# Input LayerNorm and the split of layer 0's W_IN moved from a stage of their own into the first projection stage

## What is computed

```python
hp = layer_norm(concatenate([meta, x_prompt]), in_ln_g, in_ln_b)
hs = layer_norm(x_sample, in_ln_g, in_ln_b)
for l in range(2):
    z = einsum('btd,de->bte', h, w_in[l])          # 1024 -> 1184
    cq, ckv, kr, sq, sk, sv = split(z)             # then RMS norms and rotary embedding of the parts
    # latent attention, sliding-window attention, W_OUT, LayerNorm,
    # SwiGLU FFN (2816 wide), LayerNorm
```

## Time and profile before

| | us |
|---|---|
| median of 3 runs | 3561.3 (3555.37 to 3571.3) |
| the profiled execution | 3558.67 |
| its span, first to last instruction | 3556.9 |
| PE busy | 3131.2 (88%) |
| DVE busy | 1603.1 (45%) |
| ACT busy | 847.7 (24%) |
| POOL busy | 829.7 (23%) |
| mean granted clock of PE, share of 2.4 GHz | 0.926 |

### The profile page before, as it was taken

One profiled execution on the slowest core, in us unless ns is written; L12 is line 12 of the kernel. 1 busy time (PEld: TensorE's weight loads), 2 busy tenths in 40 slices (PEclk: granted clock), 3 DMA queues, 4 the chain that ended last, 5 costly groups with the idle time before them and its releaser, 6 DMA issues. The chain is left out here.

```text
span 3556.9 us, 46203 instructions
## 1 busy us (share of the span) xinstructions
PE 3131.2 (88%) x18240; PEld 2848.6 (80%) x18240; DVE 1603.1 (45%) x2904; ACT 847.7 (24%) x1612; POOL 829.7 (23%) x675
## 2 busy tenths in 40 slices
PE   0978887889899999999859688878889999999995
PEld 0966665767899999999749566667669999999995
DVE  6447777546322222222355577756562222222226
ACT  1323333621311111111123233345121111111111
POOL 1222333621211121111012133345111211111211
PEclk9988998779999999999969898977999999999997
DMA  5221112621211011110133211045121111111101
GB/s 196 86 89 45 31 31 69 178 75 67 71 36 35 35 53 41 41 41 24 51 103 108 74 39 31 25 124 153 62 74 42 49 46 41 41 35 35 37 22 66
DMA packets 122002, 222.70 MB, mean 63 GB/s; under 512 B 33408, under 2 KB 74624, under 8 KB 121168
## 3 DMA queue, kind: packets, MB, share of 16 engines
q1 hardware_dynamic: 111072, 189.22, 16.5%
q0 software_dynamic: 10800, 31.73, 2.3%
HBM read 174.40 MB, written 42.46 MB: 61 GB/s over the span
## 5 line engine op out<-in xcount | busy, mean ns | idle before, releaser
L2166 PE MATMUL PS<-xh,fwh 128*128 128x390 f32 (+1 forms) x2112 | 719.0, 340 | 6.7 <-DVE fwl L2110 6.7
L2167 PE MATMUL PS<-xl,fwh 128*128 128x390 f32 (+1 forms) x2112 | 723.0, 342 | 0.0
L2168 PE MATMUL PS<-xh,fwl 128*128 128x390 f32 (+1 forms) x2112 | 722.1, 342 | 0.0
L2134 DVE TENSOR_TENSOR acc<-acc,PS 128x390 f32<-128x390 f32 x528 | 295.8, 560 | 494.0 <-PE PS L2168 494.0
L2121 DVE TENSOR_TENSOR gate<-PS,gate 128x390 f32<-128x390 f32 x132 | 74.4, 564 | 747.5 <-PE PS L2168 747.5
L2166 PEld LDWEIGHTS PS<-xh,fwh 128*128 128x128 f32 x2112 | 399.1, 189 | 7.5 <-issue 6.9
L2167 PEld LDWEIGHTS PS<-xl,fwh 128*128 128x128 f32 x2112 | 398.9, 189 | 0.6
L2168 PEld LDWEIGHTS PS<-xh,fwl 128*128 128x128 f32 x2112 | 398.2, 189 | 0.0
L2166 PE MATMUL PS<-hidh,fwh 128*128 128x390 f32 (+1 forms) x1056 | 358.1, 339 | 4.5 <-DVE hidl L2125 4.5
L2168 PE MATMUL PS<-hidh,fwl 128*128 128x390 f32 (+1 forms) x1056 | 359.4, 340 | 0.0
L2167 PE MATMUL PS<-hidl,fwh 128*128 128x390 f32 (+1 forms) x1056 | 358.6, 340 | 0.0
(11 more groups left out here) (430 smaller groups left out, 5540.8 us busy)
## 6 DMA issues: line engine op xcount, KB each, us to landing
raw<-in_W_FF SPq DMA_DIRECT2D x88, 512.0 KB, 3.2
fraw<-in_W_FF SPq DMA_DIRECT2D x44, 512.0 KB, 3.2
raw<-in_W_IN SPq DMA_DIRECT2D x16, 592.0 KB, 4.9
ht<-out_H SPq DMA_DIRECT2D x18, 512.0 KB, 4.9
sqt_scratch<-sqTs POOLq DMA_DIRECT2D x18, 512.0 KB, 4.3
mt<-mix_scratch SPq DMA_DIRECT2D x18, 512.0 KB, 4.5
hc<-out_H SPq DMA_DIRECT2D x18, 512.0 KB, 3.8
out_H<-yo POOLq DMA_DIRECT2D x18, 512.0 KB, 3.0
```

What stands on the lines that cost most here:

```text
L2134: dve.tensor_tensor(a, a, Tb[e % 2][:, 0:NT[i]], ALU.add).then_inc(S("f_y"), 1)
L2166: pe.matmul(out, wh, mh, start=start, stop=False)
L2167: pe.matmul(out, wh, ml, start=False, stop=False)
L2168: return pe.matmul(out, wl, mh, start=False, stop=stop)
```

## The change

- The first stage and its barrier are gone, and the buffers x0, y0 and lnp with them. Tiles of layer 0 are loaded from the input X into stage A's own ht, normed in place there, stored from there to H by POOL (layer 0's stage C reads them), and transposed from there. PE's x_T(t) of layer 0 waits for the norm's second pass of tile t. The load of tile t waits also for the store of tile t-2.
- DVE makes the norm of tile 0 ahead of x_lo(0), that of tile 1 behind the W_IN split, and in turn n the statistics of tile n+2 ahead of norm_rope(n) and its two passes behind stack_lo(n). POOL's roots and stores go into its turns accordingly.
- Layer 0's W_IN is loaded in three transfers (blocks 0 and 1, 2 to 4, 5 to 7) into w0raw, in room which cqT and the keys use later. The split of its eight blocks stands ahead of turn 0, four of them ahead of tile 0's x_hi and x_lo. PE waits for the blocks one by one in z(0, 0).
- In both layers tile 0 and tile 1 are loaded ahead of the gains and rotary tables; before, the gains came first and the tables in between.
- Some semaphores are merged (ln_stats and ln_mv to ln_parts, the two of the sinks to one, f_acc into f_y), and gains and offsets are handed to `ln_apply` as two arguments; the operations are the same.

The diff, without the merging of semaphores and the adapted calls:

```diff
@@ -347,10 +349,12 @@
         winl = m("winl", [P, KD, INW], F32R)
 
-        m = Map(after_kv)
-        x0 = [m(f"x0_{i}", [P, D]) for i in range(2)]
-        y0 = [m(f"y0_{i}", [P, D]) for i in range(2)]
-        lnp = m("lnp", [P, 2 * D])
+
+        lng = Map(wuv_at)("lng", [P, D])
+        lnb = Map(kss_at)("lnb", [P, D])
+        m = Map(after_w)
+        w0raw = m("w0raw", [P, KD, INW])
+        assert m.at <= after_kv
 
         m = Map(after_kv)
@@ -560,6 +565,21 @@
                 for place, src in it[0]:
                     sp.dma_start(place(raw[i % 2]), src).then_inc(S(f"raw{i % 2}_in"), 16)
+        W0_PARTS = ((0, 2), (2, 5), (5, KD))
+
+        def first_split_load(sp, k):
+            k0, k1 = W0_PARTS[k]
+            part = W_IN[0, k0 * P:k1 * P, :].rearrange("(k p) n -> p k n", p=P)
+            sp.dma_start(w0raw[:, k0:k1, :], part).then_inc(S(f"w0_in{k}"), 16)
+
+        def first_split_hi(act, k):
+            act.wait_ge(S(f"w0_in{[k < b for _, b in W0_PARTS].index(True)}"), 16)
+            act.activation(winh[:, k, :], w0raw[:, k, :], ACT.Copy).then_inc(S("split_hi"), 1)
+
+        def first_split_lo(dve, k):
+            dve.wait_ge(S("split_hi"), k + 1)
+            dve.tensor_tensor(winl[:, k, :], w0raw[:, k, :], f(winh[:, k, :]), ALU.subtract).then_inc(S("split_lo"), 1)
+
         def split_hi(act, l, which, part=slice(None)):
             for i, it in list(enumerate(split_items(l, which)))[part]:
                 q = first[l, which] + i
@@ -832,23 +850,27 @@
         @block.sync
         def _(sp):
-            load_params(sp, 0, "0")
-            for t in range(TILES):
-                if t >= 2:
-                    sp.wait_ge(S("ln_norm"), q0(t - 2) + 1)
-                sp.dma_start(x0[t % 2][0:rows(t), :], X[cols(t), :]).then_inc(S(f"ht_in{t % 2}"), 16)
-                if t >= 1:
-                    load_split(sp, 0, "A", slice(t - 1, t))
-            barrier(sp, 1)
             for l in range(L):
-
+                tokens = X if l == 0 else H[l]
+
+                def tile_load(t):
+                    sp.dma_start(ht[t % 2][0:rows(t), :], tokens[cols(t), :]).then_inc(S(f"ht_in{t % 2}"), 16)
+
+                tile_load(0)
+                if l == 0:
+                    sp.dma_start(lng[:, :], LNP[0:1, 0:D].to_broadcast([P, D])).then_inc(S("lnp_in"), 16)
+                    sp.dma_start(lnb[:, :], LNP[0:1, D:2 * D].to_broadcast([P, D])).then_inc(S("lnp_in"), 16)
+                    for k in range(len(W0_PARTS)):
+                        first_split_load(sp, k)
+                tile_load(1)
                 load_params(sp, l, "A")
                 for t in range(2):
-                    sp.dma_start(ht[t][0:rows(t), :], H[l, cols(t), :]).then_inc(S(f"ht_in{t}"), 16)
                     sp.dma_start(rot[t][0:rows(t), :], ROT[cols(t), :]).then_inc(S(f"rot_in{t}"), 16)
                 for t in range(2, TILES):
                     sp.wait_ge(S("a_xT"), A(l, t - 2) + 1)
-                    sp.dma_start(ht[t % 2][0:rows(t), :], H[l, cols(t), :]).then_inc(S(f"ht_in{t % 2}"), 16)
+                    if l == 0:
+                        sp.wait_ge(S(f"yo_out{t % 2}"), 16 * (t // 2))
+                    tile_load(t)
                     sp.wait_ge(S("a_rope"), A(l, t - 2) + 1)
                     sp.dma_start(rot[t % 2][0:rows(t), :], ROT[cols(t), :]).then_inc(S(f"rot_in{t % 2}"), 16)
                     if t == 3:
@@ -1034,19 +1056,22 @@
             pool.wait_ge(S("set"), set_no("ident_zero"))
             pool.affine_select(out=ident[:, :], in_=ident[:, :], compare_op=ALU.not_equal, fill=1.0,
                                base=0, pattern=[[-1, P]], channel_multiplier=1).then_inc(S("set"), 1)
-            for t in range(TILES):
+
+            def input_store(t):
+                pool.wait_ge(S("ln_out"), q0(t) + 1)
+                pool.dma_start(H[0, cols(t), :], ht[t % 2][0:rows(t), :]).then_inc(S(f"yo_out{t % 2}"), 16)
+
+            for t in range(2):
                 ln_root(pool, q0(t), rows(t))
-                pool.wait_ge(S("ln_out"), q0(t) + 1)
-                pool.dma_start(H[0, cols(t), :], y0[t % 2][0:rows(t), :]).then_inc(S(f"yo_out{t % 2}"), 16)
-            pool.wait_ge(S(f"yo_out0"), 16 * (TILES // 2))
-            pool.wait_ge(S(f"yo_out1"), 16 * (TILES // 2))
-            barrier(pool, 1)
+                input_store(t)
             for l in range(L):
                 pool.memset(f(krn[:, :, :]), 0.0).then_inc(S("set"), 1)
                 pool.wait_ge(S("set"), set_no("krn_zero", l))
                 pool.memset(f(krn[:, 1:4:2, 0:1]), 1.0).then_inc(S("set"), 1)
                 for t in range(TILES):
                     r = rows(t)
+                    if l == 0 and t + 2 < TILES:
+                        ln_root(pool, q0(t + 2), rows(t + 2))
                     pool.wait_ge(S("a_mse"), A(l, t) + 1)
                     pool.tensor_tensor(mrs[t % 2][0:r, :], mse[t % 2][0:r, :], half[0:r, 0:1].to_broadcast([r, 2]),
                                        ALU.pow).then_inc(S("a_root"), 1)
@@ -1062,7 +1087,12 @@
                             .then_inc(S("vs_out"), 16)
                     if t >= 1:
                         store_q(pool, l, t - 1)
+                    if l == 0 and t + 2 < TILES:
+                        input_store(t + 2)
                 store_q(pool, l, TILES - 1)
+                if l == 0:
+                    for i in range(2):
+                        pool.wait_ge(S(f"yo_out{i}"), 16 * (TILES // 2))
                 pool.wait_ge(S("cqT_out"), 16 * (4 * (l + 1)))
                 pool.wait_ge(S("sqT_out"), 16 * (TILES * (l + 1)))
                 pool.wait_ge(S("vs_out"), 16 * (9 * (l + 1)))
@@ -1200,8 +1230,6 @@
         @block.scalar
         def _(act):
-            split_hi(act, 0, "A")
-            barrier(act, 1)
             for l in range(L):
                 def x_hi(t):
@@ -1297,7 +1325,13 @@
                     act.activation(KSh[:, :, CH:CH + META], meta.to_broadcast([P, NCH, META]), ACT.Copy)\
                        .then_inc(S("a_meta_hi"), 1)
+                if l == 0:
+                    for k in range(4):
+                        first_split_hi(act, k)
                 x_hi(0)
+                if l == 0:
+                    for k in range(4, KD):
+                        first_split_hi(act, k)
                 for n in range(TILES + 1):
                     if n + 1 < TILES:
                         x_hi(n + 1)
@@ -1614,21 +1648,14 @@
             dve.memset(lateK[:, :], 0.0).then_inc(S("t_zero"), 1)
             dve.wait_ge(S("t_zero"), 3)
             dve.memset(lateK[CH:P, 8:9], MASKED).then_inc(S("t_zero"), 1)
-            params(dve, "0")
-            for t in range(TILES + 1):
-                if t < TILES:
+            for l in range(L):
+
+                def input_stats(t):
                     dve.wait_ge(S(f"ht_in{t % 2}"), 16 * (t // 2 + 1))
-                    ln_stats(dve, q0(t), x0[t % 2], rows(t))
-                if t >= 1:
-                    if t >= 3:
-                        dve.wait_ge(S(f"yo_out{(t - 1) % 2}"), 16 * ((t - 1) // 2))
-                    ln_apply(dve, q0(t - 1), x0[(t - 1) % 2], y0[(t - 1) % 2], lnp, rows(t - 1))
-                if t >= 1:
-                    split_lo(dve, 0, "A", slice(t - 1, t))
-            barrier(dve, 1)
-            for l in range(L):
-
-                params(dve, (l, "A"))
+                    ln_stats(dve, q0(t), ht[t % 2], rows(t))
+
+                def input_norm(t):
+                    ln_apply(dve, q0(t), ht[t % 2], ht[t % 2], lng, lnb, rows(t))
                 def x_lo(t):
                     r = rows(t)
@@ -1734,9 +1761,21 @@
                     dve.tensor_copy(KR2[:, 0:META], Tb[0][:, P:P + META])
                     meta = Tb[0][:, 2 * P:2 * P + META].rearrange("p (c n) -> p c n", c=1)
                     dve.tensor_tensor(KSl[:, :, CH:CH + META], meta.to_broadcast([P, NCH, META]),
-                                      f(KSh[:, :, CH:CH + META]), ALU.subtract).then_inc(S("a_meta_lo"), 1)
-
+                                      f(KSh[:, :, CH:CH + META]), ALU.subtract)
+
+                if l == 0:
+                    input_stats(0)
+                    dve.wait_ge(S("lnp_in"), 32)
+                    input_norm(0)
+                    for k in range(4):
+                        first_split_lo(dve, k)
                 x_lo(0)
+                if l == 0:
+                    for k in range(4, KD):
+                        first_split_lo(dve, k)
+                    input_stats(1)
+                    input_norm(1)
+                params(dve, (l, "A"))
                 for n in range(TILES + 1):
                     if n + 1 < TILES:
                         x_lo(n + 1)
@@ -1744,16 +1783,20 @@
                         post_lo(n - 1)
                     if 4 <= n < 4 + UK:
                         split_lo(dve, l, "B", slice(n - 4, n - 3))
+                    if l == 0 and n + 2 < TILES:
+                        input_stats(n + 2)
```

(52 more changed lines are left out.)

4 lines of the change are left out of this document (2 added, 2 removed).

## The result

| | before | after |
|---|---|---|
| median, us | 3563.2 (3555.4 to 3571.3, 4 runs) | 3602.2 (3595.5 to 3606.6, 4 runs) |
| the profiled execution | 3558.7 | 3601.8 |
| its span | 3556.9 | 3600.0 |
| mean granted clock | 0.926 | 0.915 |

The ratio is 1.0108, with a 95% interval of 1.0080 to 1.0136: the changed kernel is slower by 1.1%, 39 us by the medians and 43 by the profiled executions. The forecast was 3602, 1.1% more than the 3561.3 of the three runs of before known then.

What follows compares the result with a forecast made beforehand. PE was taken to bound the kernel, so only its idle and slow time counts: -52.0 - 0.9 + 79.5 + 16 = +42.6 on 3558.7 gives 3601.3, forecast as 3602 us (+1.1%), 8-in-10 range 3585 to 3617.

Steps and rivals of the forecast that it cites:

- Start, -52: Layer 0's start: without first stage and barrier, PE's x_T(1) starts at 30.6 instead of 82.6, gaining 52 us.
- Stalls, +79.5: Layer 0's projection stage: PE waits for DVE's late norm passes in eight turns, 8.69 to 11.42 us each, 79.5 total.
- Clock, +16, bounds 13 and 20: Behind each of the eight stalls PE restarts at low clock, losing 1.65 to 2.5 us each, 16 us in all.
- POOL and SP, 0 to 0.3 per turn: Layer 0's turns: POOL's extra root costs 0 to 0.3 us in each of eight; SP's wait for stores costs nothing.
- Layer 1's start, -0.9: Tile 0's load issued ahead of 192 KB of gains: 0.4 us saved for the issue, 0.5 for the bytes.
- Sum +42.6: All terms added on the profiled execution's 3558.7 us, giving 3601.3; later stages merely shifted, less 1 us in layer 1.
- Rival one: The norm is hidden in half-idle DVE's time in each turn, so the kernel gets faster, 3506 us; chance 3%.
- Rival two: The stalls are there but shorter, stalls and clock costing 70 us or less, time within 0.5%; chance 5%.
- three: The stalls come without the clock's loss behind them, 3586 us; chance 7%.
- four: Worse: start's transfers at the mean rate and longer slow stretches, or POOL's root late each turn; 3618 to 3635; 10%.

Runs made afterwards that it cites:

- mid: Changed kernel with the two norm passes of tile n+2 moved ahead of norm_rope(n), behind the statistics; 3553.7 us, ratio to before 0.9987.
- warm: Changed kernel with PE given products nobody reads in the eight stalls, to keep the clock up; 3589.5 us, ratio to before 1.0068.
- load_early: Changed kernel with SP loading layer 0's tiles a turn earlier, the norm staying where it was; 3605.4 us, ratio to before 1.0115.
- l1order: Changed kernel with the loads at layer 1's start in the order of the kernel before; 3608.3 us, a single time.
- ahead: Changed kernel with statistics and both norm passes of tile n+2 moved between x_lo(n+1) and post_lo(n-1); 3516.8 us, ratio to before 0.9865.
- ahead_load: Changed kernel with the edits of ahead and load_early together; 3511.5 us, ratio to before 0.9855.

## Why the prediction was right, step by step

- *Start, -52.* Measured -51.7. The sum was right to 0.4 us, three terms in it were not: parameters in at 8.0 instead of 6.6, part 0 of W_IN at 10.96 instead of 9.6, and part 2 at 21.13 instead of 20.1. The first two did not lie on the path, since ACT and DVE catch up while part 1 is on its way (15.57, forecast 15.5). Part 2's lateness cost DVE 0.43 us of wait for block 5 (22.35), which its splits, 1.3 us apart instead of 1.38, made up for: by luck, no term of mine. What is left of the error is POOL's root for tile 1, for which DVE waits 0.46 us (last section).
- *Stalls, +79.5.* Measured 77.6, in eight pieces as said, 8.35 for 8.69 and 10.8 to 11.3 for 10.94 to 11.42. What I had too much was 0.09 us in the start of the passes, 0.09 in the hand-over to PE (0.06, not 0.15), and 0.16 in the rotary's start (0.67 behind z(1), not 0.83). mid shows that the pieces follow the list.
- *Clock, +16, bounds 13 and 20.* Measured 18.2 in the trace, of which 16.7 are the clock by warm (12.8 by the medians) and 1.5 the end of the last product, which my sum left out. 1.8 to 3.0 us were lost per turn with it, 1.6 to 2.8 without, where I had 1.65 to 2.5. The slow stretches ran to 6.0 us (tile 8, 216.77 to 222.82), longer than the longest of my three rows (5.0), and 12 products were slow behind tile 3, where I had put 6 to 10.
- *POOL and SP, 0 to 0.3 per turn.* No wait for POOL's root shows in the turns of the changed kernel. load_early confirms it for SP.
- *Layer 1's start, -0.9.* Measured -2.6: the mis-sized term. I priced the place in the queue by bytes; what was saved is 2.2 us of landing time behind the gains, and l1order brings it back.
- *Sum +42.6.* Measured +43.1 on the profiled executions, and +39.0 between the medians. From 3601.3 the forecast went to 3602; with the median of before, 3561.3, as its base it would have been 3603.9. Either lies within the runs. That the sum was met to 0.5 us owes something to luck. The stage's end (+1.1) and turn 0 (+0.4) were at nothing in it, and so were the stages behind, which do not stay as they were: layer 1's stage B took 6.4 us more, and all the rest behind layer 0's stage A, with the 2.6 of layer 1's start, 8.9 less. Stage B of layer 1 starts at these instructions, in the kernel before and in the changed one, and the windows cover it (columns as in the earlier trace rows):

```profile
2003.99 1.11 PE L2278 MATMUL PS<-ident,raw 128*128 128x128 f32 x4 [7.14 <-POOLq L518]
...
2003.99:2352.35 348.36, 297.39 (x2131) 210.35 (x2131) 260.45 (x448) 108.50 (x178) 113.22 (x116) 0.91 0.12 37
```

```profile
2041.87 1.12 PE L2324 MATMUL PS<-ident,raw 128*128 128x128 f32 x4 [7.19 <-POOLq L522]
...
2041.87:2396.65 354.78, 303.73 (x2131) 216.20 (x2131) 260.54 (x448) 108.87 (x178) 113.14 (x116) 0.88 0.12 36
```

The matmuls are the same in number (2131); PE is busy 6.3 us longer, at a granted clock of 0.88 instead of 0.91. In the seven other profiles of this study (edits of the changed kernel) this stage takes 354.8 to 357.6 us at 0.88 to 0.89, while the same stage of layer 0 takes 343.8 to 354.6. Since there is one profile of the kernel before, it stays open whether the change lowers the clock there or whether it is scatter; the order of layer 1's loads is not what does it (l1order: 355.1).
- *Rival one* (hidden norm, 3506) was wrong for this kernel and right in its arithmetic: ahead and ahead_load, in which the norm does stand where DVE is idle, measured 3516.8 and 3511.5. The rule of the Trainium skill beside it (Perfetto Trace Analysis, Identifying the Most-Contended Engine: optimize the engine with the highest occupancy first) goes by busy time, and its ranking agrees with this trace (PE 88% of the span, DVE 45%). Busy time does not price the order, though: the runs show 85 us between two orders of the same instructions at equal busy time (3602.2 and 3516.8; DVE busy for 1603.1 us in the one and 1600.9 in the other). *Rival two* fell to the lengths of the stalls, *three* to the changed kernel's windows and to warm, and *four* did not come about.

## What to carry to other kernels

When work is given to an engine with idle time, find the idle time in that engine's list, not in its busy share: follow the list from the last thing that it has to wait for to the new step, and see who is waiting behind the new step on the other engine. Put the new step ahead of the wait, where the engine is idle, and what was a stall of 8 to 11 us per turn is free. Here a stall of 8 to 11 us on PE cost 1.6 to 2.8 us more for the clock, and stalls of only 2.65 to 3.65 us cost about 1.6, all but one. A wait made finer (block by block) brings nothing while a coarser one stands ahead of it in the same list.
